# The first FFN of a two-layer diffusion backbone: w1 and w3 as seven products of half blocks, w2 on token halves, weights as pieces in a ring

## The reference

```python
def swiglu(h, w1, w3, w2):
    return (jax.nn.silu(h @ w1) * (h @ w3)) @ w2
...
    for i in range(DEPTH):
...
        x = x + g1 * y_l
        f_l = rmsnorm(x, norm_ffn_g[i]) * (1.0 + sc2) + sh2
        x = x + g2 * swiglu(f_l, ffn_w1[i], ffn_w3[i], ffn_w2[i])
        if not last:
            h_ctx = h_ctx + cg1 * y_c
            f_c = rmsnorm(h_ctx, norm_ffn_g[i]) * (1.0 + csc2) + csh2
            h_ctx = h_ctx + cg2 * swiglu(f_c, ffn_w1[i], ffn_w3[i], ffn_w2[i])
    return rmsnorm(x, final_norm_g)
```

## Time and profile before

| what | value |
|---|---|
| median of 3 runs | 1680.38 us (1680.29 to 1681.06) |
| span of the profiled execution | 1679.1 us |
| TensorE busy | 1613.2 us, 96%, 10014 matmuls |
| TensorE weight loads | 1351.4 us, 80% |
| VectorE busy | 598.2 us, 36% |
| ScalarE busy | 520.8 us, 31% |
| GpSimd busy | 599.4 us, 36% |
| mean granted TensorE clock | 0.987 |
| DMA | 160.64 MB, mean 96 GB/s |

### The profile page before, as it was taken

One profiled execution on the slowest core, in us unless ns is written; L12 is line 12 of the kernel. 1 busy time (PEld: TensorE's weight loads), 2 busy tenths in 40 slices (PEclk: granted clock), 3 DMA queues, 4 the chain that ended last, 5 costly groups with the idle time before them and its releaser, 6 DMA issues. The chain is left out here.

```text
span 1679.1 us, 22699 instructions
## 1 busy us (share of the span) xinstructions
PE 1613.2 (96%) x10014; PEld 1351.4 (80%) x10014; DVE 598.2 (36%) x713; ACT 520.8 (31%) x577; POOL 599.4 (36%) x433
## 2 busy tenths in 40 slices
PE   6999999998899999999999999999978999999997
PEld 4888787877788888888888887788866788888886
DVE  4553333453431121111211124769987322121122
ACT  4343242322321211111101123477873321122222
POOL 2121211212142332332323334345474444555443
PEclk7999999999999999999999999999999999999999
DMA  9333334222233432333332422121213233223322
GB/s 336 97 98 105 88 90 126 76 76 76 75 101 101 120 95 87 97 105 101 101 100 76 120 82 76 51 76 56 71 50 100 76 100 101 88 90 99 100 82 82
DMA packets 200341, 160.64 MB, mean 96 GB/s; under 512 B 7234, under 2 KB 193972, under 8 KB 200244
## 3 DMA queue, kind: packets, MB, share of 16 engines
q1 hardware_dynamic: 199856, 159.08, 30.7%
q10 hardware_dynamic: 388, 0.12, 0.0%
HBM read 157.08 MB, written 2.10 MB: 95 GB/s over the span
## 5 line engine op out<-in xcount | busy, mean ns | idle before, releaser
L512 POOL TENSOR_TENSOR w_lo<-raw,w_hi 128x512 fp32r<-128x512 f32 x392 | 561.3, 1462 | 1027.9 <-ACT w_hi L1063 1027.8
L574 PE MATMUL duo<-a_hi,w_hi 128*128 128x512 f32 (+1 forms) x1584 | 466.3, 356 | 23.2 <-DVE a_lo L1544 16.2
L577 PE MATMUL duo<-a_lo,w_hi 128*128 128x512 f32 (+1 forms) x1584 | 461.0, 353 | 0.0
L580 PE MATMUL duo<-a_hi,w_lo 128*128 128x512 f32 (+1 forms) x1584 | 460.5, 352 | 0.0
L1063 ACT ACTIVATE w_hi<-raw 128x2048 fp32r<-128x2048 f32 x98 | 187.6, 1914 | 539.8 <-PE duo L580 533.8
L574 PEld LDWEIGHTS duo<-a_hi,w_hi 128*128 128x128 f32 x1584 | 257.9, 190 | 77.0 <-issue 32.2
L577 PEld LDWEIGHTS duo<-a_lo,w_hi 128*128 128x128 f32 x1584 | 257.7, 190 | 42.8
L580 PEld LDWEIGHTS duo<-a_hi,w_lo 128*128 128x128 f32 x1584 | 257.3, 190 | 42.7
L1777 DVE TENSOR_TENSOR hid<-duo,gate 128x1024 f32<-128x1024 f32 (+1 forms) x33 | 33.5, 1043 | 523.3 <-PE duo L580 523.3
L574 PE MATMUL duo<-h_hi,w_hi 128*128 128x512 f32 (+1 forms) x528 | 160.5, 356 | 0.0
L580 PE MATMUL duo<-h_hi,w_lo 128*128 128x512 f32 (+1 forms) x528 | 159.4, 354 | 0.0
(11 more groups left out here) (275 smaller groups left out, 1591.9 us busy)
## 6 DMA issues: line engine op xcount, KB each, us to landing
raw<-in_ffn_w_dram SPq DMA_DIRECT2D x120, 512.0 KB, 4.8
mod_ring<-in_w_mod_dram SPq DMA_DIRECT2D x80, 512.0 KB, 5.4
raw<-in_gla_w_in_dram SPq DMA_DIRECT2D x24, 512.0 KB, 4.8
mod_start<-in_w_mod_dram SPq DMA_DIRECT2D x8, 1024.0 KB, 12.6
raw<-in_lru_w_in_dram SPq DMA_DIRECT2D x16, 512.0 KB, 4.1
raw<-in_ffn_w_dram SPq DMA_DIRECT2D x16, 384.0 KB, 3.8
raw<-in_gla_w_out_dram SPq DMA_DIRECT2D x8, 512.0 KB, 4.9
raw<-in_lru_w_out_dram SPq DMA_DIRECT2D x8, 512.0 KB, 4.0
```

The costliest lines, as they stand in the source:

```text
L512: pool.tensor_tensor(w_lo[b][:, k:k + 2], raw[b][:, k:k + 2], w_hi[b][:, k:k + 2].bitcast(F32), ALU.subtract).then_inc(lo_ready, 1)
L574: pe.matmul(tile_out(ps, t, part, n), wh, act_hi[:, k, s:s + n], start=opens, stop=False, skip_group_check=True)
L577: pe.matmul(tile_out(ps, t, part, n), wh, act_lo[:, k, s:s + n], start=False, stop=False, skip_group_check=True)
L580: mm = pe.matmul(tile_out(ps, t, part, n), wl, act_hi[:, k, s:s + n], start=False, stop=last, skip_group_check=True)
```

## The change

Pair 0 of w1 and w3 stays as it was. The other ten pairs of each become a *dense unit*: the product of the 1024x256 weights with the 1024x768 inputs is cut into halves in each direction (4 blocks; 1 tile of 128 outputs; 384 tokens, each half with 256 latent and 128 context tokens) and made by seven products of 4 blocks x 384 tokens instead of eight (Winograd's form of Strassen's scheme). Four of the seven use sums of weight quarters (`w_sum`, S1 to S4, made by VectorE for each unit), and four use sums of input quarters (`t_hi`, `t_lo`, made once by `block_sums` and `block_low` on VectorE and `round_t` on ScalarE). The products share three banks (`PRODUCTS` names weight piece and bank), and VectorE and ScalarE move results between banks and `gate` or `hid` while the next product runs.

w2 runs in six groups of pairs (`ROW_GROUPS`: the first has one pair, the others two), one output tile at a time over all eight tiles, for each token half of 384 columns. The hidden rows of a group are held in `ha_hi`, `ha_lo` and in the freed second halves of `a_hi`, `a_lo` (`row_rounded` on ScalarE, `row_low` on VectorE).

Weights of these units are *pieces* of 128x512 (4 blocks x 128 columns; 128x256 in the first w2 group) in a ring of five slots `ring_hi`, `ring_lo`. SP loads half chunks of 512 KB into four `raw_quarter` buffers. After product g ScalarE makes the high part of piece g + 5, VectorE the sums for piece g + 6. All low parts are made by GpSimd (`BY_DVE` is empty). The last tile of the last group ends on 256 latent columns, and the squares that follow are split to fit.

```diff
+RING = 5
+ROW_GROUPS = [[0], [1, 2], [3, 4], [5, 6], [7, 8], [9, 10]]
...
+PRODUCTS = [("A11", 0), ("S2", 1), ("S1", 2), ("S3", 1), ("A12", 0), ("A22", 1), ("S4", 2)]
+SUMS = ["S1", "S2", "S3", "S4"]
+BY_DVE = ()
...
+SKIP = PIECE[("w2", 1, 5)]
+def piece_slot(g):
+    return (g if g < SKIP else g + 2) % RING
...
+            def half_load(half, src):
+                quarter_free(half)
+                rows_ = src.shape[0] // P
+                sp.dma_start(raw_quarter[quarter(half)][:, 0:rows_], src.rearrange("(k p) n -> p k n", p=P)
+                             ).then_inc(quarter_loaded[quarter(half)], 16)
...
+            for g, piece in enumerate(PIECES):
+                if piece[2] not in BY_DVE:
+                    pool.wait_ge(piece_hi, g + 1)
+                    pool.tensor_tensor(piece_rows(ring_lo, piece), piece_source(piece),
+                                       piece_rows(ring_hi, piece).bitcast(F32), ALU.subtract).then_inc(lo_by_pool, 1)
...
+            def seven_products(u):
...
+                for j, (p, b) in enumerate(PRODUCTS):
+                    lo_wait(pe, u + (p,))
+                    if j == 0:
+                        duo_wait(name)
...
+                    elif j == 1 and chunk == 0:
+                        pe.wait_ge(t_ready, 4)
+                    elif j == 3:
+                        pe.wait_ge(bank_read, 3 * chunk + 1)
+                    elif j == 4:
+                        pe.wait_ge(first_copied, chunk + 1)
+                    elif j == 5:
+                        pe.wait_ge(bank_read, 3 * chunk + 2)
+                    elif j == 6:
+                        pe.wait_ge(bank_read, 3 * chunk + 3)
...
+                    for k in range(4):
+                        pe.matmul(out_, hi[:, k], act_hi[:, k], start=j < 3 and k == 0, stop=False, skip_group_check=True)
+                        pe.matmul(out_, hi[:, k], act_lo[:, k], start=False, stop=False, skip_group_check=True)
+                        mm = pe.matmul(out_, lo[:, k], act_hi[:, k], start=False, stop=k == 3, skip_group_check=True)
+                    mm.then_inc(piece_used, 1)
...
+            def after_product(u, j):
...
+                if j == 1:
+                    dve.wait_ge(first_copied, chunk + 1)
+                    dve.tensor_tensor(c12, b, c21, ALU.add).then_inc(bank_read, 1)
+                elif j == 3:
+                    dve.tensor_tensor(c22, b, c21, ALU.add).then_inc(bank_read, 1)
+                    dve.wait_ge(bank_read, 3 * chunk + 2)
+                    dve.tensor_tensor(c22, c_, c22, ALU.add).then_inc(bank_read, 1)
...
+                elif j == 5:
+                    dve.tensor_tensor(c21, b, c21, ALU.add).then_inc(c21_made, 1)
+                    if u[0] == "w3":
+                        dve.wait_ge(c21_made, chunk + 1)
+                        dve.wait_ge(bank_read, 3 * chunk + 3)
+                        dve.tensor_tensor(hid[:, 1], hid[:, 1], gate[:, 1], ALU.mult).then_inc(hid_made, 1)
...
+            def first_ffn():
+
+                block_sums(0)
+                block_sums(1)
+                block_low(0)
...
+                dve.wait_ge(mod_turned, 13)
+                block_low(3)
+                wait_done(dve, ("w1", 0, 0))
+                for piece in PIECES[0:RING + 1]:
+                    sums_for(piece)
...
+                row_low(0, 0)
+                row_low(0, 1)
+                half_section(6, 0)
+                g = 0
+                for n, u in enumerate(UNITS):
+                    for j in range(KT if u[0] == "w2" else len(PRODUCTS)):
+                        if u != ("w2", len(ROW_GROUPS) - 1) or j < KT - 1:
+                            dve.wait_ge(piece_used, g + 1)
+                        if u[0] != "w2":
+                            after_product(u, j)
...
+                        if g + RING + 1 < len(PIECES):
+                            sums_for(PIECES[g + RING + 1])
...
+                        if j == 0 and u[0] == "w1" and UNITS[n - 1][0] == "w3":
+                            row_low(u[1] - 1, 1)
+                        if u[0] == "w3" and j == 2:
+                            half_section(6 + u[1] // 2, u[1] % 2)
+                        g += 1
```

More of the change, by code:

```diff
@@ L64, in duo_table @@
     add(*[("out", 0, n) for n in range(1, 4)])
[L66 to L73, removed]
+    add(("stat", 1), ("w1", 0, 0), ("w3", 0, 0))
+    for unit in UNITS:
+        if unit[0] == "w2":
+            begun += [("w2", 0, unit[1], t) for t in range(KT)]
+        else:
+            begun.append((unit[0], 0, unit[1]))
     add(("stat", 2), ("lu", 0), ("lu", 1))
@@ L81, in duo_table @@
     add(("out", 1, 0), ("out", 1, 1), ("stat", 3))
-    ffn(1)
+    for part, (first, n) in enumerate(FFN_PARTS):
+        for i in range(first // 2, (first + n) // 2):
+            add(("w1", 1, i), ("w3", 1, i))
+        add(*[("w2", 1, part, i) for i in range(4)])
     add(*[("fin", t) for t in range(4)])
@@ L100, in chunk_table @@
     names += [("out", 0, n) for n in range(4)]
[L102 to L110, removed]
+    names += [("w1", 0, 0), ("w3", 0, 0), ("lu", 0), ("lu", 1)]
     for n in range(BLOCKS - 1):
@@ L113, in chunk_table @@
     names.append(("lg", BLOCKS - 1))
-    names += [("out", 1, n) for n in range(4)] + ffn(1)
+    names += [("out", 1, n) for n in range(4)]
+    for part, (first, n) in enumerate(FFN_PARTS):
+        for i in range(first // 2, (first + n) // 2):
+            names += [("w1", 1, i), ("w3", 1, i)]
+        names += [("w2", 1, part, i) for i in range(4)]
     return {name: i for i, name in enumerate(names)}
@@ L452, in ffn_loads @@
                         columns(("w2", layer, part, i), w2, 256 * i, rows=n)
[L453 to L457, removed]
+            first_ffn_loads()
             def gate_columns(n):
@@ L518, in _ @@
                                    ALU.subtract).then_inc(lo_ready, 1)
[L519 removed]
+            for ch in range(1, CH[("lu", 0)]):
+                low(ch)
+            for g, piece in enumerate(PIECES):
[3 more added lines that the diff above has]
+                                       piece_rows(ring_hi, piece).bitcast(F32), ALU.subtract).then_inc(lo_by_pool, 1)
+            for ch in range(CH[("lu", 0)], CH[("out", 1, 1)]):
                 low(ch)
@@ L1786, in ffn @@
                                           ALU.subtract).then_inc(hid_ready, 1)
[L1788 to L1792, removed]
+                        dve.wait_ge(hid_ready, HID[part] + j + 1)
+                    residual_loop(("w2", layer, part), layer, 5, parts)
@@ new lines, in add_down, with after_down @@
+            def add_down(group, t, part, cols, banks=slice(0, 2)):
+                x_ = halves_of(part, xres[:, t])
+                ps = duo(("w2", 0, group, t))[:, banks, HL:HT] if part else duo(("w2", 0, group, t))[:, banks, 0:HL]
+                return dve.scalar_tensor_tensor(out=x_[:, cols], in0=ps, scalar=mod[:, 5, t, part:part + 1],
+                                                in1=x_[:, cols], op0=ALU.mult, op1=ALU.add)
+            def after_down(group, t):
+                name, every = ("w2", 0, group, t), slice(0, 2)
+                if t == 0:
+                    dve.wait_ge(mod_ready, 6)
+                steps.mark(add_down(group, t, 0, every))
+                moved(add_down(group, t, 1, every), name)
+                wait_moved(dve, name)
```

477 lines of the change are left out of this document (440 added, 37 removed).

## The result

The changed kernel takes 1702.58 us (median of 4 runs, 1700.89 to 1703.3), the kernel before, beside it, 1680.72 us (4 runs, 1680.29 to 1681.38). The ratio is 1.0124, 95% interval 1.011 to 1.0139: slower by 1.2%. The forecast was 1637 us, faster. The profiled execution has a span of 1699.2 us. In all that follows, one execution resembles no other of its kernel (2229.14 us at a granted clock of 0.652, in the fourth experiment): no ratio contains it.

What follows compares the result with a forecast made beforehand. TensorE's matmul issue was taken to bound the first FFN. Span 1679.1 - 51.5 (columns, w2) + 2 (banks) + 4 (start) + 2 (end) = 1635.6 us; median of runs 1637 us, range 1629 to 1660.

Steps and rivals of the forecast that it cites:

- The step that failed: SP's queue in the dense units: waiting adaLN pieces still let each half load issue some 19 us before its sum; cost nothing.
- a lower granted clock after a stall: Listed sign that the forecast is wrong: the granted clock falls after a stall; no size given.
- Columns: TensorE's dense units: 384-column matmuls at 173.3 ns, a unit 14.56 us in place of 16.96, 48.0 us saved over twenty.
- the rival's 176.7: Rival: 384-column matmuls take 176.7 ns, half a mixed pair; 9 us less saving, about 1646 us; chance 12%.
- GpSimd: Low parts in dense units: seven pieces at 1.29 us are 9.0 us of 15.8; capacity is there, even with the lock.
- the 2.57 at which the rival decides: Rival: GpSimd becomes the bound from 2.57 us a low part on; at 2.81 us about 1713 us, slower; chance 7%.
- The Trainium skill's rule cited in the prediction: Two-input VectorE SBUF work and GpSimd lock a shared port pair per instruction; 27.3 of 31.6 us per two units, fits.
- VectorE's banks: Dense units: VectorE reads each bank in time, tightest behind a w3 unit's third product by 0.2 us; 2 us allowed.
- The start: Before the fourth product of the first dense unit, TensorE waits for VectorE to read the first bank; 4 us charged, bounds 1 and 10.
- The end: Last w2 stretch covering the squares shrinks from 4.1 to 1.4 us of matmuls; 2 us charged, bounds 0 and 3.
- The dense units: Twenty chunks of w1 and w3 become dense units: 48.0 us saved, before 2 us for banks and 4 for the start.
- w2: w2 splits 768 columns as 384 + 384: 528 pairs at 346.7 ns in place of 353.3, 3.5 us saved.

Runs made afterwards that it cites:

- the fourth experiment: Against the changed kernel: adaLN pieces issued ahead of the next unit's half loads, and low parts A11 and A12 made by VectorE; 1641.14 us, ratio 0.9759.

## Why the prediction was wrong, step by step

**The step that failed** is the sentence "SP's queue blocks on adaLN pieces until the unit two before is done, and still issues each half some nine products (19 us) before its sum: nothing." It asks whether half loads come late behind adaLN pieces that wait. It does not ask the reverse: whether adaLN pieces come late behind half loads that wait. At five places they do, and the cost is not nothing but 57.0 us of span (1699.2 - 1642.2), shown by changing the order alone and, in proportion, at two places. 42.9 us of it are the waits. At the place shown, 8.9 us of waiting came with 10.0 us more to the first w2 matmul and 1.05 more in the eight steps after it: the other 2 us of such a place are matmuls at the lower clock. Over all five places the way from the last product to the first w2 matmul is 48.6 us longer than with the order repaired, and the slow steps behind it make most of the rest. No rival named it; the list of what would show the forecast wrong had "a lower granted clock after a stall", which came, at places not foreseen.

With the order repaired, the other steps can be read from that kernel.

- **Columns: right within a unit.** From 574.74 to 576.82 twelve steps of 384 columns take 2.08 us, 173.3 ns each, the value forecast, and not the rival's 176.7. Two slots of adaLN pieces, one unit apart in the kernel with the order repaired:

```profile
724.11 1.08 PE L832 MATMUL mod_psum<-mod_ring,cs 128*32 128x128 f32 x32
739.91 1.08 PE L832 MATMUL mod_psum<-mod_ring,cs 128*32 128x128 f32 x32
```

 This unit with its slot takes 15.80 us; forecast were 14.56 + 1.2 = 15.76. With a turn it is more, up to 16.43. Whole units cost a little more than their steps, see the account below.
- **GpSimd: right.** In the kernel after, its low parts of loaded pieces in the first FFN (ns min/median/max) and one of VectorE's four weight sums, the slowest:

```profile
L700 POOL TENSOR_TENSOR ring_lo<-raw_quarter,ring_hi x108: 724/1287/2421, 488.0 to 1038.1; 128x512 fp32r<-128x512 f32 x100, 128x256 fp32r<-128x256 f32 x8
```
```profile
L2238 DVE TENSOR_TENSOR w_sumS<-w_sumS,raw_quarter x20: 692/1596/1792, 491.0 to 999.9; 128x512 f32<-128x512 f32 x20
```

 The median is 1.29 us, as in the earlier trace rows, the worst 2.42, under the 2.57 at which the rival decides. This sum tells of the shared lock: 0.69 us in the six of twenty that ran beside no instruction of GpSimd, 1.59 to 1.79 in the fourteen others. The Trainium skill's rule cited in the prediction (page SBUF — State Buffer, section "SBUF: two separate sides") agrees with these rows; it did not decide the time.
- **VectorE's banks: better than charged, and late elsewhere.** 2 us were allowed, with the w3 units as the tight place. There TensorE waits for no bank. But in five w1 units the fourth product begins 0.2 us late: in the one from 643.40 on VectorE splits hidden rows of the pair before (2.04 us from 647.24), reads the bank from 649.20 to 649.74, and the product that needs it begins at 649.89. That is 1 us in all.
- **The start: mechanism right, size 4 us forecast, 4.9 measured.** The wait is 3.1 us and stands where it was put, before the fourth product; the rest, 1.5 us or so at the lower clock, was not in the sum.
- **The end: 2 us forecast, 2.4 measured.** TensorE's timeline of the kernel with the order repaired, its last w2 matmul and the last sum of squares, and then the last sum of squares of the kernel before (its last w2 matmul is in the earlier trace rows):

```profile
1002.59 0.28 PE L1179 MATMUL duo<-a_hi,ring_lo 128*128 128x256 f32 x1
...
1007.11 1.06 PE L875 MATMUL duo<-sq,ones 128*128 128x256 f32 x2
```
```profile
1044.70 1.12 PE L686 MATMUL duo<-sq,ones 128*128 128x512 f32 x2
```

 1007.11 - 1002.59 = 4.5 us, against 1044.70 - 1042.57 = 2.1.

**The account.** Forecast span 1635.6; the order's 57.0 and 6.6 more make 1699.2. The 6.6 us can be read from TensorE's timelines, from start to start, of the kernel before and of the one with the order repaired.

- The dense units: forecast 48.0 us saved, less 2 for banks and 4 for the start, 42.0. The twenty chunks before took 339.8, the twenty units 299.9: 39.8 saved, 2.2 less. The first unit takes 19.58, the other nineteen 14.56 to 14.90, 14.75 in the mean for 84 x 173.3 ns = 14.56; beside the late banks, the steps at a unit's edges to an adaLN slot are longer (0.28 and 0.27 us in place of 0.17 in the unit from 627.61 on; the four units that stand between a later w2 group and a turn take 14.56).
- w2: forecast 3.5 us saved, measured 0.7 lost. To its last matmul it took 184.5 us before and takes 185.2 now. This term was mis-sized: it prices all of w2's pairs at the 353.3 ns of the earlier trace rows, but the second part of w2 in the kernel before took 66.67 us for 192 pairs, 347.2 each, which leaves next to nothing to save. In the kernel with the order repaired a whole group takes 33.41 us for 192 matmuls, 174.0 each, and the first group 17.50 for 96, with a wait of 0.5 for `xres`. The second part of w2 in the kernel before, its first row and the first behind it, and then the row that follows the group begun at 578.10:

```profile
816.08 0.61 PE L574 MATMUL duo<-h_hi,w_hi 128*128 128x512 f32 x2
...
882.75 0.51 PE L574 MATMUL duo<-a_hi,w_hi 128*128 128x512 f32 x2
```
```profile
611.50 0.33 PE L1156 MATMUL duo<-a_hi,ring_hi 128*128 128x384 f32 x1
```

- The end: 0.4 us more than forecast.

Together 6.8 us; the rest of the kernel gives back 0.2. No run changed the edges of the units or w2, so why they cost what they do stays open.

## What to carry to other kernels

For an issue queue that works in order, ask two things of every issue: what it makes late when it waits, and what waits ahead of it; a buffer ring that looks only a few pieces ahead can tie the second answer to the engine that will need the data. When the work between two loads in such a queue is changed, walk the queue once around each place where the pattern breaks (here the w2 groups), not only through the regular stretch. A cheap sign in the profile is a wait for a DMA that was issued only when the engine was already idle: here fewer bytes took 1.2 us from a place of some 9, another order took all of it.

## What was not expected of the hardware

A short wait costs more than itself. After idle stretches of 6 to 9 us, and after one of only 3.1 us, TensorE's matmuls of 384 columns ran 0.32 us apart in place of 0.17, for 1.9 to 4.5 us at the five places and for 3.2 us at the start; the granted clock read 0.50 behind the wait shown and 0.54 behind the short one. Per place, 8.6 us of waiting (42.9 / 5) became 11.4 us of span (57.0 / 5), and the start's 3.1 became 4.9.
